# The samples' part of a delta rule on TensorE: 32-column and 32-row products in place of 128-column and padded 512-column ones

## What is computed

```python
def step(S, xs):
    q_c, k_c, u_c, w_c, gc_c, att_c = xs
    v_new = u_c - jnp.einsum('bhck,bhkv->bhcv', w_c, S)
    o = (jnp.einsum('bhck,bhkv->bhcv', q_c * jnp.exp(gc_c)[..., None], S)
         + jnp.einsum('bhij,bhjv->bhiv', att_c, v_new))
    g_last = gc_c[..., -1]
    S = (S * jnp.exp(g_last)[..., None, None]
         + jnp.einsum('bhck,bhcv->bhkv', k_c * jnp.exp(g_last[..., None] - gc_c)[..., None], v_new))
    return S, o
```

## Time and profile before

| | us |
|---|---|
| median of 3 runs (1769.43 to 1771.33) | 1769.63 |
| the profiled execution's own time | 1769.2 |
| its span, first to last instruction | 1766.9 |
| PE busy | 1730.6 (98%) |
| VectorE busy | 1123.8 (64%) |
| ScalarE busy | 468.7 (27%) |
| GpSimd busy | 253.7 (14%) |
| granted TensorE clock, mean | 0.999 |

### The profile page before, as it was taken

The page is one execution under the profiler, slowest core; times in us unless marked ns, Lnnn a source line. Parts: engine busy times, 40 slices in busy tenths (PEclk is TensorE's granted clock), DMA queues, the critical chain, the costliest instruction groups (busy, mean ns, idle before and its releaser), DMA issues. The chain is left out here.

```text
span 1766.9 us, 21908 instructions
## 1 busy us (share of the span) xinstructions
PE 1730.6 (98%) x7699; PEld 1353.9 (77%) x7699; DVE 1123.8 (64%) x2212; ACT 468.7 (27%) x1108; POOL 253.7 (14%) x540
## 2 busy tenths in 40 slices
PE   8999999998989999999999999999899999999999
PEld 5777779985767777777777777777677777777777
DVE  4766778859776666763337655567766676642365
ACT  2433406633332222220005101113322222200051
POOL 0111116644210000000110000002100000001100
PEclk9999999999999999999999999999999999999999
DMA  4232220024112222232121222221122222322211
GB/s 152 72 112 85 80 60 13 5 105 155 48 59 81 75 72 84 83 130 102 66 89 45 96 72 82 83 62 48 48 83 84 72 72 84 127 90 91 73 61 54
DMA packets 45642, 139.34 MB, mean 79 GB/s; under 512 B 4944, under 2 KB 12240, under 8 KB 45536
## 3 DMA queue, kind: packets, MB, share of 16 engines
q1 hardware_dynamic: 42864, 133.36, 22.9%
q10 hardware_dynamic: 2672, 4.61, 0.8%
HBM read 129.63 MB, written 8.31 MB: 78 GB/s over the span
## 5 line engine op out<-in xcount | busy, mean ns | idle before, releaser
L274 PE MATMUL bank<-z,ring 128*128 128x288 f32 x1952 | 507.2, 407 | 7.4 <-DVE z L392 2.8
L274 PEld LDWEIGHTS bank<-z,ring 128*128 128x128 f32 x1952 | 370.0, 190 | 113.7 <-issue 5.1
L274 PE MATMUL bank<-x,ring 128*128 128x288 f32 x1632 | 428.5, 409 | 9.9 <-DMA x<-in_x 4.7
L274 PEld LDWEIGHTS bank<-x,ring 128*128 128x128 f32 x1632 | 310.5, 191 | 100.8 <-issue 7.3
L2081 DVE SCALAR_TENSOR_TENSOR scratch<-scratch 128x592 f32<-128x592 f32 x176 | 146.3, 832 | 25.5 <-ACT scratch L2025 23.8
L274 PE MATMUL bank<-y,ring 128*128 128x288 f32 x616 | 156.6, 406 | 2.0 <-DVE x L1842 2.0
L274 PEld LDWEIGHTS bank<-y,ring 128*128 128x128 f32 x616 | 117.0, 190 | 34.7 <-issue 2.4
L274 PE MATMUL bank<-big,ring 128*128 128x288 f32 x536 | 135.1, 407 | 2.7 <-issue 1.1
L274 PEld LDWEIGHTS bank<-big,ring 128*128 128x128 f32 x536 | 101.4, 190 | 32.3 <-issue 3.4
L2025 ACT ACTIVATE scratch<-scratch 128x592 f32<-128x592 f32 x88 | 69.4, 789 | 91.0 <-DVE scratch L2055 89.5
L2115 POOL COPY scratch<-scratch 128x2 f32<-128x2 f32 x88 | 26.4, 300 | 466.0 <-ACT scratch L2011 466.0
(11 more groups left out here) (374 smaller groups left out, 2377.5 us busy)
## 6 DMA issues: line engine op xcount, KB each, us to landing
ring<-in_w_up SPq DMA_DIRECT2D x88, 512.0 KB, 3.5
ring<-in_w_scin SPq DMA_DIRECT2D x24, 512.0 KB, 3.5
ring<-in_w_qkv SPq DMA_DIRECT2D x21, 512.0 KB, 3.5
ring<-in_w_down SPq DMA_DIRECT2D x12, 704.0 KB, 4.2
scratch<-in_w_down SPq DMA_DIRECT2D x12, 704.0 KB, 5.4
ring<-in_w_z SPq DMA_DIRECT2D x8, 512.0 KB, 3.5
big<-in_st_S SPq DMA_DIRECT2D x16, 256.0 KB, 5.9
out_dn_S_sample<-big SPq DMA_DIRECT2D x16, 256.0 KB, 2.6
```

What stands on the lines that cost most here:

```text
L274: last = pe.matmul(bank[:, 0:HALF], w[:, k * P:(k + 1) * P], rhs(k), start=start and k == 0, stop=k == self.depth - 1, skip_group_check=no ...
```

## The change

Four edits, all in the samples' part:

1. **Selectors by 32 columns.** states_pe issues 16 products of each head in place of 8, each with 32 stationary columns (four samples of k or of q). Each writes 32 partitions of the bank: x = 0, 1 (k, q) and r = 0, 1 (samples 0 to 3, 4 to 7) name the quarter 2x + r; the innermost loops go through the four quarters. The selector slots shrink from 1024 to 640 columns.
2. **The last decay goes into k.** keys_act makes, per head, four copies of k scaled by the last decay (64 x 512, into Y) on ScalarE, before the new values are there; LAST_S holds the scales (two copies of 32 x 32 on VectorE). values_dve and decayed_act go, and with them the three memsets of the padding.
3. **The update by 32 rows.** update_pe issues 8 products of each head: 32 partitions (r = 0 or 1, alternating), 128 stationary columns of the scaled k, 128 moving columns of S_VNEW. The two halves go to two banks, which UPDATE_BANKS reuses for several heads.
4. **Order.** Both halves of a head are updated together, head after head, on all engines; values of heads 0 to 5 come before the prompt's turn; transposes and gates go by four heads.

```diff
         def states_pe(self, pe, h):
             pe.wait_ge(self.state_in[h], 32)
             pe.wait_ge(self.sel, 2 * h + 2)
-            for b in range(NB):
-                last = pe.matmul(BANK[h][:, P:2 * P], sel_window(h, b), states(h, b // SH)[:, b % SH, :],
-                                 start=b == 0, stop=b == NB - 1)
+            for i in range(SH):
+                for r in range(2):
+                    for x in range(2):
+                        last = pe.matmul(BANK[h][sample_quad(2 * x + r), P:2 * P], sel_window(h, SH * r + i, x),
+                                         states(h, r)[:, i, :], start=i == 0, stop=i == SH - 1)
             last.then_inc(self.ks, 1)
...
-        def update_pe(self, pe, h, r):
...
-            pe.matmul(BANK[h][:, :], S_KTOK[:, h, :], decayed(h, r), start=True, stop=True).then_inc(self.su, 1)
+        def update_pe(self, pe, h):
+            pe.wait_ge(self.keyed, h + 1)
+            for b in range(SH):
+                for r in range(2):
+                    part = sample_quad(r)
+                    last = pe.matmul(BANK[UPDATE_BANKS[h][r]][:, b * P:(b + 1) * P], keys(h)[part, b, :],
+                                     S_VNEW[part, h, :], start=True, stop=True)
+                    if b == SH - 1:
+                        last.then_inc(self.su, 1)
...
+            for h in range(FILL[-1] + 1):
+                self.values_pe(pe, h)
             pe.wait_ge(self.prompt.scaled, NCH)
...
             pe.wait_ge(self.prompt.gated, (NCH - 1) * H + 1)
             self.states_pe(pe, 6)
+            for h in range(GROUP):
+                self.outputs_pe(pe, h)
             pe.wait_ge(self.prompt.gated, (NCH - 1) * H + 2)
             self.states_pe(pe, 7)
-            for h in first:
-                self.outputs_pe(pe, h)
...
+            self.values_pe(pe, 6)
+            self.values_pe(pe, 7)
+            pe.wait_ge(self.o_sq, 2)
+            self.update_pe(pe, 0)
+            pe.wait_ge(self.o_sq, 4)
+            self.update_pe(pe, 1)
+            for h in range(GROUP, H):
+                self.outputs_pe(pe, h)
+            pe.wait_ge(self.s_out, nth_update(0, 1))
+            self.update_pe(pe, 2)
...
-        def values_dve(self, dve, h):
-            dve.wait_ge(self.vn, h + 1)
-            dve.tensor_tensor(decayed(h, 0)[A], S_VNEW[A, h, :].unsqueeze(1).to_broadcast([SAMP, SH, P]),
-                              S_DEC[A, h, last_tok][:, 0:SH].unsqueeze(2).to_broadcast([SAMP, SH, P]),
-                              ALU.mult).then_inc(self.vb0, 1)
...
+            for r in range(2):
+                part = sample_quad(r)
+                dve.tensor_copy(LAST_S[part], S_DEC[part, :, last_tok][:, :, SH * r:SH * (r + 1)]
+                                ).then_inc(self.last, 1)
...
-        def decayed_act(self, act, h):
-            act.wait_ge(self.vn, h + 1)
-            act.wait_ge(self.prompt.gated, (NCH - 1) * H + 2)
-            for b in range(SH, NB):
-                last = act.activation(decayed(h, 1)[A, b - SH, :], S_VNEW[A, h, :], ACT.Copy,
-                                      scale=S_DEC[A, h, NS * b + NS - 1:NS * b + NS])
-            last.then_inc(self.vb1, 1)
+        def keys_act(self, act, h):
+            for b in range(SH):
+                last = act.activation(keys(h)[:, b, :], S_KTOK[A, h, :], ACT.Copy, scale=LAST_S[A, h, b:b + 1])
+            last.then_inc(self.keyed, 1)
...
         def pool(self, pool, stored):
...
             self.select_pool(pool, 7)
-            self.decay_pool(pool, 3, 0)
-            pool.wait_ge(self.prompt.gated, (NCH - 1) * H + 2)
-            pool.wait_ge(self.sdec, GROUP)
-            pool.memset(Z[B, :, 0:SH * P], 0.0).then_inc(self.pad, 1)
...
+            for h in range(3, 6):
+                self.decay_pool(pool, h)
+            pool.wait_ge(self.sdec, nth_update(5, 1))
             self.scale_pool(pool, 0)
+            self.decay_pool(pool, 6)
+            pool.wait_ge(self.sdec, nth_update(6, 1))
             self.scale_pool(pool, 1)
+            self.decay_pool(pool, 7)
```

More of the change, by code:

```diff
@@ L759, in outputs_pe, with turn_pe @@
                           skip_group_check=True).then_inc(self.o, 1)
-            def update_pe(self, pe, h, r):
[L762 to L769, removed]
-                pe.matmul(BANK[h][:, :], S_KTOK[:, h, :], decayed(h, r), start=True, stop=True).then_inc(self.su, 1)
[L772 to L775, removed]
+            def update_pe(self, pe, h):
[7 more added lines that the diff above has]
+                            last.then_inc(self.su, 1)
+            def turn_pe(self, pe, group):
+                pe.wait_ge(self.scaled, group + 1)
+                for h in range(group * GROUP, (group + 1) * GROUP):
+                    last = pe.transpose(BANK[group][:, h % GROUP * SAMP:(h % GROUP + 1) * SAMP], S_OS[B, h, :], IDENT[B, B])
+                last.then_inc(self.o_turned, 1)
             def pe(self, pe):
@@ L942, in act @@
                                    ).then_inc(self.tok, 1)
-                for group in (range(GROUP), range(GROUP, H)):
-                    for h in group:
-                        self.values_act(act, h)
-                    for h in group:
-                        self.outputs_act(act, h)
-                    for h in group:
-                        self.decayed_act(act, h)
+                act.wait_ge(self.last, 2)
+                act.wait_ge(self.tok, 2 * H)
+                for h in range(H):
+                    self.keys_act(act, h)
+                for h in range(FILL[-1] + 1):
+                    self.values_act(act, h)
+                for h in range(GROUP):
+                    self.outputs_act(act, h)
+                for h in range(FILL[-1] + 1, H):
+                    self.values_act(act, h)
+                for h in range(GROUP, H):
+                    self.outputs_act(act, h)
             def select_pool(self, pool, h):
@@ L1037, in store @@
             def store(self, sync):
-                for group in range(0, H, GROUP):
+                for h in range(H):
                     for r in range(2):
-                        for h in range(group, group + GROUP):
-                            sync.wait_ge(self.s_out, updates(h, r))
-                            store(sync, O["dn_S_sample"][h, :, SH * r:SH * (r + 1)], states(h, r))
+                        sync.wait_ge(self.s_out, nth_update(h, r))
+                        store(sync, O["dn_S_sample"][h, :, SH * r:SH * (r + 1)], states(h, r))
         class ConvQKV:
```

149 lines of the change are left out of this document (65 added, 84 removed).

## The result

| | before | changed |
|---|---|---|
| median of the runs, us | 1769.93 | 1755.14 |
| lowest to highest | 1769.43 to 1771.33 | 1754.06 to 1755.24 |
| the profiled execution's own time | 1769.2 | 1754.06 |
| its span | 1766.9 | 1752.3 |

The ratio is 0.9917 [0.9903, 0.993]: 14.8 us faster. (One disturbed execution of the changed kernel, with a mean granted clock of 0.594, is left out.) The same kernel, run twice more among the experiments, gave 0.992 [0.9905, 0.9935] and 0.993 [0.9918, 0.9943]. The forecast was -6.8.

What follows compares the result with a forecast made beforehand. PE was taken to bound the levels, VectorE the last stretch. States unchanged at 1.98 us with updates at 1.0 ended the stage at 410.8 against 417.61: -6.8, forecast 1762.4 us, range 1755.5 to 1772.

Steps and rivals of the forecast that it cites:

- The bounds of before: In the stage's levels and states 6 and 7 PE is the bound; in the last stretch VectorE, 21.9 of 22.6 us.
- The block of states: States on PE: 16 products half overlapped take 1.98 us per block, as before; lower end 1.2, upper end 3.77.
- The updates: Updates on PE, per head: 1.0 us if row groups half overlap, 1.85 if not; 128-column weight loads spoke against 1.0.
- case 2: Quarters and row groups on PE both overlap and pay in full: -12.8 us, 1756.4; chance 0.16.
- case 1: On PE one of the two overlaps, states or updates, pays and the other not: about -7 us, 1762.4; chance 0.38.
- the walk: Step-by-step timing of the stage from the levels' end at 389.5 us to its last engine: 410.8 or 416.5 against 417.61.
- VectorE: Last stretch: eight L842 go, 10.6 us; two gates at about 0.5; adds stay at 0.61; two added copies cost nothing.
- Case 3: Last stretch: the removed VectorE work is hidden by PE, which becomes the bound; -1.1 us, 1768.1, no change; chance 0.26.
- Case 4: States' quarters run one after another on PE: +13.2 us (chance 0.16), or +7.5 with updates overlapped (0.04).
- ScalarE: 32 copies at 0.30 us move from the last stretch to 369 to 379 us, where ScalarE is mostly idle: free.
- GpSimd: Three memsets go; 16 decays stay, at 1.04 us alone and 1.48 beside VectorE; the chain just fits.
- SyncE: Stage end: same 16 stores, the last issued right at the end; next products' weights already in the ring, cost nothing.

Runs made afterwards that it cites:

- both orders spoilt: Changed kernel with four state products of a quarter in a row and four update products of a row group in a row; 1775.81 us, ratio 1.0034.

## Why the prediction was wrong

**The bounds of before: right.** PE in the levels, VectorE in the last stretch, as the earlier trace rows had it. The levels end at 382.77; the six blocks in them account for 6 x 0.97 = 5.8, and the 1.0 of L1529 for the rest of the 6.74.

**The block of states: the step that failed.** The prediction reasoned that both records of a product go to the same quarter, that "if records start in program order, only the second record of one product and the first of the next can run side by side", and took 1.98. Measured: 1.01, below even the lower end of 1.2. The premise about the quarter was right (109 ns per record of one quarter), the one about the start was not: in the changed kernel records start in groups of four within 20 ns, and with two products of a quarter in a row, where by the reading above three records of a quarter wait, a block still takes 1.06. Nor do records start in program order: in the run with four products of a quarter in a row the 297 ns record of the next quarter is the sixth to start, ahead of three of the first quarter's eight. Weight loads overlap running matmuls too: all 16 products have the same 128 rows, and inside a block a weight load starts 2 ns behind a matmul whose record lasts 272. By the pace of one quarter, 32 records would take 32 x 0.109 = 3.49 us, 3.5 times the 1.01 of four. The lower end was wrong too, for its 0.19 of entering and leaving the shape: eight groups at 0.109 are 0.87, which leaves 0.14, and the 0.032 per record, read from products one behind the other, was no limit: inside a group of four they follow each other at 7 ns.

**The updates: the right value, too small a chance.** 1.0 was the lower end, 0.96 to 0.99 was measured. What I held against it, that records with 128 weight columns follow each other at over 0.06, read the wrong row: the two row groups load at the same time, in pairs 7 ns apart and 112 ns to the next. The time of a load does go with its columns in these traces, not with its rows: a load of 32 rows x 128 columns lasts 187 ns, one of 128 x 128 columns 192, one of 128 rows x 32 columns 110. But it doesn't follow that two groups can't load side by side.

So case 2, "both pay in full", came true, at a chance of 0.16, and case 1 was forecast at 0.38. The forecast of -6.8 lacked about the 6.0 that case 2 gives the blocks, and 1.5 more for the block below its lower end. The two prices hung on the same question, whether neighbours in different parts of the array run together, and I treated a yes to one and a no to the other as the likeliest: one cause should have had one chance. Case 2's own sum was -12.8. Against the stage's -13.86 it is short by 8 x 0.19 = 1.5 for the blocks, and the last store gave 0.7 back; the sum is then -13.6, and with the 1.0 of L1529 in that execution -14.6 of its -15.1. The median stands 0.4 below the low end of the range, which was set from -12.8 and an error of the walk of 0.9: the lower end of the block was taken as a floor, and a range should have gone below it.

**VectorE: right.** Eight L842 gone, the two gates 0.48 each (forecast about 0.5), adds at 0.62. The copies of LAST_S cost nothing. **Case 3**, that PE takes the place of what leaves VectorE, was a sound mechanism: with the 128-column blocks and the update's rows in turn 1.0018 [1.0009, 1.0027], +2.9 us against its -1.1. But that run had the lower clock for 20.5 us, which case 3 did not reckon with, so its price is not tested cleanly. **Case 4**, slower, has a run: with both orders spoilt 1.0034 [1.0018, 1.005], +6.5 us against its +7.5 to +13.2. The loops' order decides which case it is.

**ScalarE: right.** 32 copies at 0.30 from 368.33, in the levels, and nobody waits for them. **GpSimd: right.** 1.03 per decay, in the last pair too, and no add waits for one; the 1.48 seen beside VectorE before doesn't return.

**SyncE: wrong.** The last store was costed at nothing, because the next stage's first products find their weights in the ring. True, but the stage ends when every engine has issued its last instruction, and this issue is now behind the last add: 0.47 from the last engine's end to PE's next product became 1.17 after VectorE's.

**The granted clock: not in the prediction.** It falls to 0.50 at 399.3 for 6.8 us, while PE makes its last updates and then waits 2.8 us for VectorE and SyncE:

```profile
399.30:406.10 6.80, 3.98 (x18) 2.96 (x15) 5.50 (x10) 0.00 (x0) 0.17 (x1) 0.50 0.77 290
406.10:415.00 8.90, 8.90 (x38) 6.96 (x37) 8.76 (x23) 0.82 (x2) 0.00 (x0) 1.00 0.81 293
```

PE's lead on before shrinks by it from 14.9 to 13.5 at 425 us of the old time, and is 14.9 again from 432 on: PE had idled 1.99 us for VectorE (L1842) there, now 0.55. In this execution the slower clock costs the changed kernel nothing in the end, and the gain survives to the end of the program at 14.65.

## What to carry to other kernels

Small products that differ in their 32 output columns or their 32 rows ran side by side on TensorE here (16 in 1.01 us, 8 in 0.99), and the price was then the longest chain of one quarter or row group, 0.11 us per record of 128 moving columns at a granted clock of 1.00, not the number of products: write the innermost loop through the quarters, and leave no more than two float32 products of one quarter in a row (two cost a block 0.05 us here, four 1.4). Relief of one engine pays only as far as the next one lets it: compute both ends, and where two terms rest on the same unknown, give them one chance.

## What was not expected of the hardware

- **Two products of a quarter in a row cost almost nothing, four do.** Two (four records) took 1.06 us per block, four (eight records) 2.39, two quarters in turn 1.47, all quarters in turn 1.01. Places for three waiting records, each quarter's own, fit the distances; that is my estimate from these four orders.
- **The granted clock fell under a busy PE.** With the update's rows in turn it fell at 394.5, 3.7 us after the first of these products, with PE busy 3.70 of 3.70 us before and 11.5 of 11.5 after, and stayed at 0.50 for 23.9 us. With both orders spoilt it was 3.2 us and 23.9, with the old selectors and rows in turn 4.9 and 20.5. With alternating rows it came 7.8 to 10.5 us after the first and lasted 6.8 or 10.2 us. With the old update (only the selectors changed) there was 3.4 us of it, in the next stage. So long falls came behind 32-row products alone; more than that the runs don't show.
- **L1529** at 2.68 or 4.46 us in different executions, worth 1 us of the whole time, cause open.
